# Input projection as seven products on halves of tokens and of K, and the gate columns moved into the key/value stage

## What is computed

```
h = rmsnorm(x) * (1 + scale(c)) + shift(c);  gate(c) = third part of c @ ada_w + ada_b
u = h @ w_in      # q 1024 | 6 x 128 key/value | 48 branch gates | conv h, B, C 3 x 1024 | z 2048
o_attn = compressed + selected + window attention, mixed by sigmoid gates
y_conv = B * causal_conv3(C * h_c)
y = rmsnorm(x + gate * ([o_attn * silu(z_a), y_conv * silu(z_c)] @ w_out))
```

## Time and profile before

| | |
|---|---|
| runs | 1554.61 us median of 3 (1551.36 to 1560.05) |
| span of the profiled execution | 1556.0 us; no other time is given for it |
| TensorE busy, mean granted clock | 1486.5 us (96%), 0.985 |
| VectorE (DVE), ScalarE (ACT), GpSimd (POOL) busy | 692.7, 621.4, 199.9 us |
| instructions | 25222 |

### The profile page before, as it was taken

One profiled execution on the slowest core, in us unless ns is written; L12 is line 12 of the kernel. 1 busy time (PEld: TensorE's weight loads), 2 busy tenths in 40 slices (PEclk: granted clock), 3 DMA queues, 4 the chain that ended last, 5 costly groups with the idle time before them and its releaser, 6 DMA issues.

```text
span 1556.0 us, 25222 instructions
## 1 busy us (share of the span) xinstructions
PE 1486.5 (96%) x9878; PEld 1293.1 (83%) x9878; DVE 692.7 (45%) x1790; ACT 621.4 (40%) x1304; POOL 199.9 (13%) x378
## 2 busy tenths in 40 slices
PE   4899999999999999998999998998998999899998
PEld 1799999999999999997777776776776776688886
DVE  2541222323131312216677666666667655653226
ACT  2331111121111111115557777777777765641111
POOL 1100000001102100003011131131131132000000
PEclk8899999999999999999999999999999999999999
DMA  8814343235325243209721121111111019973231
GB/s 334 144 53 164 99 119 96 67 92 125 105 45 163 80 116 86 65 31 312 223 87 30 35 66 42 28 42 42 28 42 42 28 33 362 257 238 95 82 98 35
DMA packets 169061, 164.59 MB, mean 106 GB/s; under 512 B 52780, under 2 KB 150316, under 8 KB 163760
## 3 DMA queue, kind: packets, MB, share of 16 engines
q1 hardware_dynamic: 155136, 97.26, 23.5%
q0 software_dynamic: 13808, 65.73, 12.4%
HBM read 131.27 MB, written 35.83 MB: 107 GB/s over the span
## 4 chain that ended last, share of the span: by engine, by line
PE 85%; DMA 5%; DVE 4%; SPq 3%; ACT 2%; issue 1%; POOL 0%; DVEq 0%; ACTq 0%
PE PS L1025 36%; PE PS L1386 11%; PE PS L1192 8%; PE PS L1157 7%; PE PS L1136 5%; PE PS L1137 3%; PE PS L1077 2%; DMA kb<-in_cache_k_slc,idxs 1%; DMA adaw<-in_ada_w 1%; DMA xb<-in_x_prompt 1%; PE PS L989 1%; PE PS L990 1%; PE PS L991 1%; PE PS L1239 1%; SPq L535 1%
## 5 line engine op out<-in xcount | busy, mean ns | idle before, releaser
L1025 PE MATMUL PS<-hhi,wh 128*128 128x352 f32 x1152 | 250.6, 326 | 0.6 <-ACT kvt L1434 0.6
L1025 PE MATMUL PS<-hhi,wl 128*128 128x352 f32 x1152 | 248.3, 323 | 0.0
L1025 PE MATMUL PS<-hlo,wh 128*128 128x352 f32 x1152 | 248.0, 323 | 0.0
L1025 PEld LDWEIGHTS PS<-hhi,wh 128*128 128x128 f32 x1152 | 195.4, 189 | 4.5 <-issue 3.0
L1556 ACT ACTIVATE pr<-PS,nm 128x640 f32<-128x640 f32 (+7 forms) x256 | 181.2, 709 | 44.5 <-DVE nm L1908 42.1
L1025 PEld LDWEIGHTS PS<-hhi,wl 128*128 128x128 f32 x1152 | 197.8, 188 | 0.0
L1025 PEld LDWEIGHTS PS<-hlo,wh 128*128 128x128 f32 x1152 | 195.6, 188 | 0.0
L1579 ACT ACTIVATE ptt<-PS 128x512 f32<-128x512 f32 x264 | 149.7, 601 | 43.9 <-PE PS L1157 43.6
L1157 PE MATMUL PS<-ident,pr 128*128 128x128 f32 x1056 | 147.4, 274 | 0.0
L1192 PE MATMUL PS<-ptt,kvt 128*64 128x256 f32 x1056 | 137.2, 391 | 0.0
L1775 DVE TENSOR_TENSOR wl<-wr,wh 128x1024 fp32r<-128x1024 f32 x48 | 58.5, 1219 | 168.2 <-ACT wh L1470 167.7
(11 more groups left out here) (318 smaller groups left out, 2194.5 us busy)
## 6 DMA issues: line engine op xcount, KB each, us to landing
wr<-in_w_in SPq DMA_DIRECT2D x32, 512.0 KB, 5.9
adaw<-in_ada_w SPq DMA_DIRECT2D x8, 1024.0 KB, 10.1
wr<-in_w_in SPq DMA_DIRECT2D x32, 256.0 KB, 3.8
qb<-q_stacked SPq DMA_DIRECT2D x32, 256.0 KB, 3.1
mr<-mixed SPq DMA_DIRECT2D x16, 512.0 KB, 3.9
mixed<-ych POOLq DMA_DIRECT2D x8, 528.0 KB, 3.4
z_attn_silu<-zab POOLq DMA_DIRECT2D x8, 528.0 KB, 2.9
xb<-in_x_prompt POOLq DMA_DIRECT2D x8, 512.0 KB, 4.8
```

The lines of the kernel that those rows point to most:

```text
L1025: ins = pe.matmul(PS[:, bank + c, 0:CH], a[kind % 2][:, k, :], b[:, k, c * CH:(c + 1) * CH], start=(k == 0 and b is hhi and a is wh), stop ...
```

## The change

The weight blocks are now worked in pairs (the kinds C+h, B+z_c, z_a+q), 24 pairs. The tokens are cut into two halves of 528 (512 prompt and 16 sample each), K into two halves of 512, and a pair of blocks by two halves of K by two halves of tokens is a 2x2 by 2x2 product of blocks.

- The first three pairs (`NPLAIN`) do it in the plain way, 8 products each. The other 21 do it by Strassen's seven products. A product is 4 parts of K by 3 terms by 2 banks = 24 matmuls of 264 columns into a pair of banks.
- The activation operands are seven: four blocks of h and three sums; two more sums replace two of the blocks. Each of five sums is made in 4 pieces (`PIECES`) during the first three pairs: POOL adds the low parts, DVE adds the high parts and the two sums, ACT rounds, DVE forms the low part.
- For each fast pair DVE adds or subtracts five times on the raw weights, ACT rounds seven operands and DVE forms seven low parts (five slots, `NSLOT`). ACT copies two products out of PSUM and DVE does eight additions of 528 columns (`joined`) to make the four outputs. The steps behind (u, taps, silu, q) are the same, now for each token half.
- SP loads a pair of blocks (1 MB) at once into two raw tiles; `load_w(n)` waits until the last operand of the pair before is made.
- The gate columns stand in the key/value stage: `gates(s - 1)` behind each `kv(s)`. There is one buffer `gw` instead of four; its loads stand on SP behind `load_w(0)`, each behind the gates before it. The projection waits for the addition to `gate` (`ada_ev`).
- The convolution's tails are turned once, after the projection, by 8 transposes.
- The memory plan is new. The compression stage's first weights, rows and gathers are no longer fetched during the projection but at its end.
- The key/value stage has three PSUM banks instead of four; its results lie in two tiles (`kvc`, `kvt`).
- `mixed` and `z_attn_silu` in HBM are cut by token halves; the loads of the sample columns are two DMAs instead of one.

The diff's core:

```diff
+H = TOK // 2
+HT = S // 2
+HS = SAMP // 2
+HK = KC // 2
+NBLK, NPLAIN, NSLOT = 24, 3, 5
@@ SP
+            def load_w(n):
+                if n:
+                    sp.wait_ge(w_lo, operand0(n))
+                for a, kind in enumerate(KINDS[n % 3]):
...
+            load_w(0)
+            for k in range(KC):
+                if k:
+                    sp.wait_ge(ada_mm, KC + k)
+                else:
+                    sp.wait_ge(ada_mm, KC)
+                    sp.wait_ge(h_ev, 1)
+                sp.dma_start(gw[:, :], ada3[:, k, 2 * D:3 * D]).then_inc(adaw_ld[k % 4], 16)
+            for n in range(1, NBLK):
+                load_w(n)
+            sp.wait_ge(*made(NBLK - 1, 2))
+            for q in range(4):
+                load_w1(0, q)
+            sp.wait_ge(xz, 1)
+            sp.wait_ge(kc_st, 32)
+            for r in range(4):
+                load_rows(0, r)
@@ POOL
+            def gather_quarter(c, q):
+                if c == 0 and q < 2:
+                    po.wait_ge(*made(NBLK - 1, 1 if q == 0 else 4))
...
@@ PE
             for s in range(1, NTT):
                 kv(s)
+                gates(s - 1)
...
+            FAST = (O22, O11, 6, 1, O21, 0, O12)
...
+            def multiply(n, k, op, q, first, last):
...
+                w, b = wsl[(operand0(n) + k) % NSLOT], bo[op]
+                pe.wait_ge(w_lo, operand0(n) + k + 1)
+                for kk in range(HK):
+                    for x, y in ((0, 0), (0, 1), (1, 0)):
+                        for c in range(2):
+                            ins = pe.matmul(PS[:, 2 * q + c, 0:H // 2], w[:, x, kk, :], b[:, y, kk, c * H // 2:(c + 1) * H // 2],
...
@@ ACT and DVE, which operands are prepared at step i of pair n
+        def prepared_at(n, i):
+            if plain(n):
+                return EARLY_PREP.get((n, i), ())
+            own, following = operand0(n), operand0(n + 1)
+            if i < 3:
+                return (own + 4 + i,)
+            ahead = {5: (following, following + 1), 6: (following + 2, following + 3)}.get(i, ())
@@ DVE, fast pair
+            def ev_fast(n, i):
...
+                    joined(n, 2, er, ca[1], ALU.subtract)
+                    joined(n, 2, eg, ca[0], ALU.subtract)
+                if i == 4:
+                    dve.wait_ge(*dve_at(n, "w1"))
+                    joined(n, 3, ca[1], ca[1])
+                    joined(n, 3, eg, eg)
...
+                if i == 5:
+                    joined(n, 4, ca[0], ca[0])
+                    joined(n, 4, er, er)
+                if i == 6:
...
+                    joined(n, 5, er, er)
```

More of the change, by code:

```diff
@@ new lines, in piece, with raw, is_sum, sums_to @@
+        def piece(n, k):
+            return ((0, 1), (1, 1), (0, 0), (1, 0))[k] if plain(n) else {3: (0, 0), 4: (1, 1)}.get(k)
+        def raw(a, k2):
+            return wr[a][:, HK * k2:HK * k2 + HK, :]
+        def is_sum(m):
+            n, k = operand_of(m)
+            return not plain(n) and k not in (3, 4)
+        def sums_to(m):
+            return sum(is_sum(x) for x in range(m + 1))
+        def source(m):
+            n, k = operand_of(m)
+            return wsum[(sums_to(m) - 1) % 2][:, :, :] if is_sum(m) else raw(*piece(n, k))
@@ new lines, in dve_at, with made, accumulator, acc @@
+        def dve_at(n, name):
+            return p2_dve, place(DVE_EV, n, name)
+        def made(n, i):
+            return p2_mm, product(n, i) + 1
+        C11, C21, C12, C22 = range(4)
+        def accumulator(n, out):
+            return (out + 2 * (n % 2)) % 4
+        def acc(n, out):
+            q = 2 * accumulator(n, out)
+            return PS[:, q:q + 2, 0:H // 2]
+        def ring_pair(n, i):
+            return (2 + 7 * (n - NPLAIN) + i) % 4
+        def pm(n, i):
+            q = 2 * ring_pair(n, i)
+            return PS[:, q:q + 2, 0:H // 2]
@@ L537, in load_rows @@
                     sp.dma_start(xp4[c][32 * r + NPB:32 * r + NPB + 1, :, g, :], flat(pe_, 2 * r * HD, [(0, 1), (8 * HD, 8), (1, P)])).then_inc(xp_ld[c], 16)
[L539 to L566, removed]
+            load_w(0)
[15 more added lines that the diff above has]
+                load_rows(0, r)
+            sp.wait_ge(*made(NBLK - 1, 6))
+            sp.wait_ge(w_lo, N_OPERANDS)
+            sp.wait_ge(ych_st, 32 * 8)
+            sp.wait_ge(q_st, 128 * 8)
             sp.wait_ge(xz, 2)
@@ L1008, in _, with gates @@
             pe.wait_ge(tb_ev, 2)
+            def gates(k):
+                pe.wait_ge(adaw_ld[k % 4], 16 * (k // 4 + 3))
+                for c in range(4):
+                    ins = pe.matmul(PS[32 * c:32 * c + 9, 2, 0:256], vcol[:, k, 0:9], gw[:, 256 * c:256 * c + 256], start=(k == 0), stop=(k == KC - 1))
+                ins.then_inc(ada_mm, 1)
             kv_sample()
@@ new lines, in _ @@
+            pe.wait_ge(ada_ev, 8)
+            for n in range(NBLK):
+                for i in range(products(n)):
+                    if plain(n):
+                        k, op, out = PLAIN[i]
+                        if i < 4 and n:
+                            pe.wait_ge(*emptied(n - 1, former(out)))
+                        multiply(n, k, op, accumulator(n, out), i < 4, i >= 4)
+                    else:
+                        pe.wait_ge(*pair_emptied(n, i))
+                        if n == NPLAIN and i >= 2:
+                            pe.wait_ge(op_lo, {2: 4, 3: 8, 4: 16, 5: 12, 6: 20}[i])
+                        multiply(n, i, FAST[i], ring_pair(n, i), True, True)
@@ L1495, in _ @@
+            for m in range(4):
+                high(m)
             kv_evac(NTT - 1, 0)
```

774 lines of the change are left out of this document (528 added, 246 removed).

## The result

The changed kernel takes 1595.81 us (median of 4 runs, 1591.77 to 1599.78), the kernel before 1554.54 beside it: ratio 1.0265, 95% interval 1.0232 to 1.0298. It is **41 us slower**, where 17 less were forecast. The profiled execution took 1591.77 us, its span is 1590.0, against the 1556.0 of before: 34.0 to account for.

A forecast was written before the change was run, and what follows sets the result against it. TensorE, busy for all 566.1 us of the projection, was taken as the bound. Terms of -59.8 + 20 + 9 + 1 + 13 = -16.8 on 1556.0 gave 1539.2, forecast as a median of 1538 us, range 1512 to 1574.

The forecast's parts named there:

- what the matmuls are worth: Projection: 4104 matmuls of 264 columns at 0.122 us each take 500.7 us, 59.8 less than before.
- the chain rival: Projection: load, sums, rounding and low part set the pace, 9 us per group, total 1592; chance 0.28.
- the gate columns: Key/value stage: TensorE waits for `gw` until 81 us, projection starts at 156.8; net +20 us (17 to 24).
- the end: Projection's end: row loads land 18 us after it, with some waits given back; +13 us (+6 to +24).
- VectorE and the weight loads: Projection's fast pairs: VectorE barely fits, 1.3 us lost per group of three pairs; +9 us (0 to 40).
- The first three pairs: Plain pairs: VectorE's 60 us of work fits beside TensorE's 70.3 us; +1 us (0 to 10).
- The stall that was worked out: Fast pairs: the load after B+z_c starts at 12.2 us, operands are ready at 21.8 against 20.5; 1.3 us per group.
- Costed at nothing, since each has room: Projection's fast pairs: ScalarE, the PSUM pairs and the stores were each given no cost.
- The clock: Half clock after idling: about 1.9 us priced after the gate gap, 1.3 us at the projection's end.
- The weight chain: Slower rival in the projection: a 1 MB load takes 12 us instead of 7.3, 63 us in all; chance 0.28.
- GpSimd's sums hold VectorE back: First three pairs: GpSimd's additions stop VectorE, first fast pair up to 20 us late, total 1558; chance 0.10.
- own test of being wrong in kind: Met if the projection is not at least 35 us shorter than 566, or the gap at 56 is missing.

The follow-up runs named there:

- gates_ahead: Changed kernel with the first gate weights loaded ahead of the bias rows, which are written in eight pieces behind the gate loads; 1570.16 us, ratio 1.0107 to before.
- noload: Changed kernel without the weight loads after the sixth pair, later pairs reusing the sixth's weights; 1549.54 us, ratio 0.9965 to the kernel before.
- pool_writes_zero: Changed kernel with GpSimd's 20 sums of token low parts replaced by writes of zero; 1595.44 us, one run.
- load_held: Changed kernel with each weight load, from the seventh pair on, held until product 4 of the pair before is done; 1642.08 us, one run.
- windows_spread: Changed kernel with the two 2 MB window copies cut into 16 of 0.25 MB, one at each of pairs 6 to 21; 1572.78 us, ratio 1.0133 to before.
- early_sums: Changed kernel with a pair's last two weight sums made at product 0 and the next load issued sooner; 1563.92 us, ratio 1.0048 to before.

## Why the prediction was wrong

**Right: what the matmuls are worth.** 0.1222 us in a stream of 3192, where 0.122 was taken: 501.6 us for 4104, 0.9 off. The loads of the weights fit under it. (15 steps in 2.42 us are 0.1613 each, not 0.1617, and 5 to 6 us per group in the chain rival give 1564 to 1571, not 1565 to 1575; neither slip moves the verdict.)

**Right: the gate columns.** `gw` at 80.3 (81 forecast), projection at 158.15 (156.8): 21.3 us net, where 20 stood in the sum. gates_ahead gave back 26.

**Nearly right: the end.** A gap of 24.1 instead of 18, 7.4 given back instead of 5: 17 against +13. That it hangs on what else is in the DMA engines was said; that it would swing between 18 and 34 us from kernel to kernel was not.

**Wrong: "VectorE and the weight loads", +9 (0 to 40), and with it "The first three pairs", +1 (0 to 10).** The projection was put at 511 us and took 556.6. The 55.0 above 501.6 are 41.5 idle and 13.5 in which TensorE is busy: some 11 of these are the lower clock, the rest is the last matmul of each of 17 rows, which counts in full (0.28 instead of 0.12). The step that failed is the cost of the feeding loop: it was laid beside TensorE's period for the B+z_c pair alone, on an undisturbed load, and at full clock.

- *The stall that was worked out* (one in three pairs, after B+z_c) was sized well: seven gaps of 0.51 to 3.45 us, 11.6 together, where 9 stood in the sum. (VectorE was done with the B+z_c pairs 4 and 7 after 14.4 us, not 12.2.) Its picture holds too, but for more pairs. The pair from 434.98 to 456.60, a pair z_a and q, in the changed kernel's timelines of VectorE and SyncE:
```profile
446.81 0.69 DVE L2098 TENSOR_TENSOR wsl<-wsum,wsl 128x512 fp32r<-128x512 f32 x1 [0.77 <-ACT wsl L1706]
...
447.54 66.18 SPq L687 DMA_DIRECT2D wr<-in_w_in  x10
...
454.30 1.29 DVE L2092 TENSOR_TENSOR wsum<-wr 128x512 f32<-128x512 f32 x2 [2.97 <-DMA wr<-in_w_in]
```

  12.5 us from the pair's start to the last low part and the issue, 6.8 to the first sum, 2.3 more for sums, rounding and low part make 21.6, against a pair of 20.7. So pairs that were given no stall have one as well: four of them, 5.4 us together, beside the two below.
- *The transfers beside it*: the stores stand under "Costed at nothing, since each has room", and the two window copies in the same queue are not named. They are in the kernel before as well, where a load behind one took 18.5 us and harmed nothing. Here the gaps behind them are 7.14 and 8.73, 15.9 us, and both went when the copies were moved. The change did not add the copies; it took away the time that had hidden them.
- *The clock* was priced for the gate gap and forgotten for the stalls: some 11 us of the 55. In noload, without the stalls, the busy time fell by 8.4 (506.7 instead of 515.1).
- *The plain pairs* lost 8.6 us instead of 1: the sum of VectorE's work fits into TensorE's 70 us, but its order seems not to: 6.4 us of the gaps end with VectorE's low part of q (`qp`, L2157), which empties an accumulator and stands in its list behind further token sums and weight parts. That order was not changed in any run, so this cause is argued. Some 3 to 4 of the 8.6 went with GpSimd's sums in pool_writes_zero. The term's range (0 to 10) holds the 8.6.

**The rivals.** The weight chain did set the pace. Its mechanism is what the runs show; that its total of 1592 lies 4 us from the measured one is in part luck, for its price is differently made: not 12 us for each load but a long one beside each of two copies, small gaps at eleven other pairs, and the half clock. It had 0.28, and the forecast, which carried a seventh of its price (9 of 63 us), 0.36. "No slack by design" stood there as the argument for it; that sentence deserved more than 0.28, since a chain that fills its period has no way to make up for a disturbance. "GpSimd's sums hold VectorE back" is real, at 8 us of VectorE and not 20. By the rule of the Trainium skill quoted in the prediction (SBUF — State Buffer, "Who interferes with whom") the trace agrees: an operation that meets a sum ends behind it, as at 169.97, and one reached 2244 ns, 1.54 more than its 704, over a sum of 1.34. The whole cost less than feared because few of the sums met VectorE at work.

The prediction's own test of being wrong in kind was met: the projection is 9.5 us shorter, not 35. Of the 51 us by which the sum missed the profiled time, 45 are this term. With it as forecast the time would be some 1551, about where noload came out (1549.5) and just below the kernel before.

## What to carry to other kernels

When a change makes the fastest engine's work shorter, first lay the feeding loop beside the new period: last use of the buffer, issue, landing, first sum, rounding, first use. If that comes to the period or more, every neighbour transfer and every late operation is paid nearly in full (1.9 of some 2 us in load_held), however low the engines' busy shares are (VectorE 73%, DMA 34% here). Free the buffer earlier before making anything faster: two additions moved ahead by one and two products, with a narrower wait on the load, were worth 32 us here. And look up which big transfers the old slack was hiding, and which waits were harmless only because the next stage was far away.

## What the runs showed that was not expected

- A weight load's 512 KB landed 5.1 us after its issue (median of six in 430 to 520 us); the two issued 3 us behind the 2 MB copy on GpSimd's queue took 7.8 and 14.1. The Trainium skill (DMA: Bandwidth & Descriptors, "Queues, rings and completion order") has each DMA engine take turns between queues by the packet. With a copy of long rows against a load of short ones that would put the load behind, and the two landings agree in direction. It is not the whole: between 376 and 382 the copy's queue moved 1.6 MB and the load's 0.5, then both stood almost still for 2 us, and the load's other half moved only from 384 to 389. What held it there is open, and no run varied the row length alone.
- After idling 7.1 us TensorE came back at half of its clock (1.2 GHz), as the windows behind 338.77 show (PEclk 0.50, then 0.69 as a mean of both levels; from 345 on it is 1.00):

```profile
338.77:342.00 3.23, 3.23 (x15) 3.23 (x16) 2.43 (x5) 0.78 (x2) 0.00 (x0) 0.50 0.00 0
342.00:345.00 3.00, 3.00 (x19) 3.00 (x19) 2.83 (x6) 1.25 (x3) 0.00 (x0) 0.69 0.00 0
```

  That pair took 22.95 us instead of 20.68. After gaps of about 2 us both were seen: 20.66 after the 2.65 in front of 286.79 and 22.20 after the 1.98 in front of 309.43.
- The gap for the rows was 22.0, 20.4, 18.4, 20.1, 23.2, 34.4 and 28.7 us in kernels whose code there is the same (the changed kernel, noload, windows_spread, gates_ahead, load_held, early_sums, pool_writes_zero). It does not follow what was gained in front of it: noload gained 39 us and has 20.4, early_sums gained 38 and has 34.4. So a single run's gain before that gap is not yet a gain of the whole.
